# First attention: the order of the pairs' norms and of the last probabilities, and other banks

## The reference

```python
proj = x @ w_in
qa, ka, va, qb, kb, vb = split(proj)
qa, ka, qb, kb = rms_norm of each head (64 wide)
oa = dilated_mixture_attention(qa, ka, va, slopes[:8])        # 8 heads of 64
ob = differential_attention(qb, kb, vb, slopes[8:], lam)      # 4 heads; softmax 1 - lam * softmax 2
ob = rms_norm(ob, b_sub_norm) * (1.0 - lam_init)
y = concatenate([oa, ob]) @ w_out
```

## Time and profile before

| | |
|---|---|
| median of 3 runs | 2827.79 us (2825.66 to 2828.16) |
| time of the profiled execution | 2825.41 us |
| its span | 2823.6 us |
| PE busy in the span | 2793.2 us, 99% |
| DVE, ACT and POOL busy | 44% each |

### The profile page before, as it was taken

The page is one execution under the profiler, slowest core; times in us unless marked ns, Lnnn a source line. Parts: engine busy times, 40 slices in busy tenths (PEclk is TensorE's granted clock), DMA queues, the critical chain, the costliest instruction groups (busy, mean ns, idle before and its releaser), DMA issues.

```text
span 2823.6 us, 32514 instructions
## 1 busy us (share of the span) xinstructions
PE 2793.2 (99%) x12994; PEld 2267.7 (80%) x12994; DVE 1243.2 (44%) x2085; ACT 1231.8 (44%) x1805; POOL 1232.8 (44%) x549
## 2 busy tenths in 40 slices
PE   9999999999999999999999999999999999999998
PEld 8776888888878888887777888888877778888887
DVE  5666552544665525327666432021266574320112
ACT  4665442434754334334674443133345744342331
POOL 4222444444554444443455444444434564444442
PEclk9999999999999999999999999999999999999999
DMA  4212323233223332332222323333332222333332
GB/s 152 89 57 64 97 90 105 91 103 97 90 82 105 97 97 91 104 97 83 76 68 83 104 91 98 97 96 98 104 90 75 68 82 90 97 97 97 97 97 75
DMA packets 74215, 259.23 MB, mean 92 GB/s; under 512 B 9344, under 2 KB 9344, under 8 KB 74064
## 3 DMA queue, kind: packets, MB, share of 16 engines
q1 hardware_dynamic: 72768, 255.05, 29.0%
q10 hardware_dynamic: 1296, 2.10, 0.2%
HBM read 254.95 MB, written 2.13 MB: 91 GB/s over the span
## 4 chain that ended last, share of the span: by engine, by line
PE 94%; DVE 3%; ACT 2%; POOL 1%; issue 1%; DMA 0%; DVEq 0%; ACTq 0%; POOLq 0%
PE ps L427 27%; PE ps L429 27%; PE ps L428 27%; PE ps L493 2%; PE ps L523 2%; PE ps L549 1%; PE ps L506 1%; PE ps L551 1%; PE ps L550 1%; PE ps L475 1%; PE ps L477 1%; PE ps L476 1%; PE ps L438 1%; POOL w_lo L1988 0%; DVE pbuf L1457 0%
## 5 line engine op out<-in xcount | busy, mean ns | idle before, releaser
L1988 POOL TENSOR_TENSOR w_lo<-raw,w_hi 128x1024 fp32r<-128x1024 f32 x469 | 1132.9, 2418 | 1473.9 <-ACT w_hi L907 1473.8
L427 PE MATMUL ps<-xs,w_hi 128*128 128x512 f32 x2176 | 861.7, 396 | 1.6 <-DVE xs L1392 1.6
L429 PE MATMUL ps<-xs,w_lo 128*128 128x512 f32 x2176 | 847.1, 389 | 0.0
L428 PE MATMUL ps<-xs,w_hi 128*128 128x512 f32 x2176 | 847.0, 389 | 0.0
L907 ACT ACTIVATE w_hi<-raw 128x1024 fp32r<-128x1024 f32 x470 | 494.2, 1052 | 598.6 <-PE ps L429 555.6
L427 PE MATMUL ps<-hid,w_hi 128*128 128x512 f32 x1320 | 517.4, 392 | 7.7 <-DVE hid L1377 3.5
L429 PE MATMUL ps<-hid,w_lo 128*128 128x512 f32 x1320 | 514.4, 390 | 0.0
L428 PE MATMUL ps<-hid,w_hi 128*128 128x512 f32 x1320 | 514.2, 390 | 0.0
L427 PEld LDWEIGHTS ps<-xs,w_hi 128*128 128x128 f32 x2176 | 408.5, 188 | 101.1 <-issue 11.4
L428 PEld LDWEIGHTS ps<-xs,w_hi 128*128 128x128 f32 x2176 | 408.6, 188 | 88.7 <-issue 5.2
L429 PEld LDWEIGHTS ps<-xs,w_lo 128*128 128x128 f32 x2176 | 408.4, 188 | 85.5
(11 more groups left out here) (230 smaller groups left out, 2614.8 us busy)
## 6 DMA issues: line engine op xcount, KB each, us to landing
raw<-in_weights SPq DMA_DIRECT2D x470, 512.0 KB, 3.5
btab<-in_rel SPq DMA_DIRECT2D x8, 256.0 KB, 3.8
out<-tmp ACTq DMA_DIRECT2D x8, 256.0 KB, 2.0
hT<-in_x SPq DMA_DIRECT2D x3, 512.0 KB, 7.8
btab<-in_heads SPq DMA_DIRECT2D x6, 256.0 KB, 3.8
tmp<-in_heads SPq DMA_DIRECT2D x6, 256.0 KB, 4.1
common<-in_fixed SPq DMA_DIRECT2D x1, 642.0 KB, 11.0
hT<-in_x SPq DMA_DIRECT2D x2, 256.0 KB, 3.7
```

What stands on the lines that cost most here:

```text
L427: pe.matmul(banks[bank][:], wh, rh, start=(k == 0), stop=False)
L428: pe.matmul(banks[bank][:], wh, rl, start=False, stop=False)
L429: last = pe.matmul(banks[bank][:], wl, rh, start=False, stop=(k == len(specs) - 1))
L1988: gp.tensor_tensor(w_lo[:, n % NPAIR, :], raw[:, n % NRAW, :], w_hi[:, n % NPAIR, :].bitcast(F32), ALU.subtract).then_inc(*w_low.tick(n))
```

## The change

The edit is in the list of steps alone; no instruction is added or dropped.

- `before0`: `qk_turn` of pairs 0 and 1 comes ahead of the last `qk` step of the next pair.
- Pairs 3 to 7: the root is put at the end of the block before (`behind0[2]`, `[5]`, `[9]`, `[17]`, `[21]`), the norm is the first of the `beside` part in blocks 3, 6, 10, 18 and 22, ahead of the block's `qk` or `vb` step. The transposes stay in blocks 4, 7, 11, 19 and 23.
- `pair_banks` of pairs 4 to 7, `vb_banks` and `out_banks` are other banks.
- The `sublow` of unit 6, due in block 33, comes after `turn` and `unturn` of block 31 (`held`).
- The output matmuls (0 to 2, chunk 6) move behind `mix` of unit 7, those of (3 and 4, chunks 5 and 6) behind its `submean`.

```diff
--- before.py
+++ after.py
@@ -276,14 +276,15 @@
                 if 0 <= n - 1 < n_blocks:
                     steps.append(("weigh", n - 1))
                 steps += beside.get(n, [])
-                steps += due
+                held = due if n == n_blocks + LAG - 1 else []
+                steps += [] if held else due
                 if n >= LAG:
                     steps.append(("turn", n - LAG))
                     if late is not None:
                         steps.append(("mix", late))
                         later += ends_of(stage, late)
                         late = None
-                    steps.append(("unturn", n - LAG))
+                    steps += [("unturn", n - LAG)] + held
                     if (n - LAG) % NB == NB - 1:
                         late = (n - LAG) // NB
                 steps += (behind or {}).get(n, [])
@@ -305,42 +306,53 @@
 
 
         pairs = [(0, 0), (1, 0), (0, 1), (1, 1), (2, 0), (3, 0), (2, 1), (3, 1)]
-        pair_banks = [(5, 6), (7, 2), (5, 6), (7, 4)] + [((6, 7), (5, 6), (7, 5))[p % 3] for p in range(4)]
-        vb_banks = {(0, 0): 7, (0, 1): 6, (1, 0): 5, (1, 1): 6}
+        pair_banks = [(5, 6), (7, 2), (5, 6), (7, 4), (5, 6), (7, 5), (6, 7), (5, 6)]
+        vb_banks = {(0, 0): 6, (0, 1): 5, (1, 0): 7, (1, 1): 5}
 
         def unit_steps(p):
             return [("qk", (p, i, j)) for i in range(2) for j in range(2)]
 
         def vb_steps(half):
             return [("vb", (half, i, j)) for i in range(2) for j in range(2)]
-
-        def behind_next(p, after):
-
-            return [[after[0], ("qk_root", p)], [("qk_norm", p), after[1], ("qk_turn", p)], [after[2]], [after[3]]]
 
         before0 = unit_steps(0)
         for p in range(2):
             after = unit_steps(p + 1)
-            before0 += after[:1] + [("qk_root", p), ("qk_norm", p)] + after[1:] + [("qk_turn", p)]
+            before0 += after[:1] + [("qk_root", p), ("qk_norm", p)] + after[1:3] + [("qk_turn", p)] + after[3:]
+
+
+        beside0, behind0 = {}, {}
         after = unit_steps(3)
-        parts0 = [[after[0]], [after[1], ("qk_root", 2)], [("qk_norm", 2), after[2]], [after[3], ("qk_turn", 2)]]
-        for p, after in ((3, unit_steps(4)), (4, unit_steps(5)), (5, vb_steps(0))):
-            parts0 += behind_next(p, after)
-        parts0 += [[f] for f in unit_steps(6)] + behind_next(6, unit_steps(7))
-        beside0 = {}
-        for i, part in enumerate(parts0):
-            beside0.setdefault(0 if i < 2 else i - 1 if i < 6 else i - 2, []).extend(part)
+        beside0[0] = [after[0], after[1], ("qk_root", 2)]
+        beside0[1] = [("qk_norm", 2), after[2]]
+        beside0[2] = [after[3], ("qk_turn", 2)]
+        for p, n, after in ((3, 3, unit_steps(4)), (4, 6, unit_steps(5)), (5, 10, vb_steps(0))):
+            behind0[n - 1] = [("qk_root", p)]
+            beside0[n] = [("qk_norm", p), after[0]]
+            beside0[n + 1] = [after[1], ("qk_turn", p)] + ([after[2]] if p == 3 else [])
+            beside0[n + 2] = [after[2 if p > 3 else 3]]
+            if p > 3:
+                beside0[n + 3] = [after[3]]
+        for i, f in enumerate(unit_steps(6)):
+            beside0[14 + i] = [f]
+        after = unit_steps(7)
+        behind0[17] = [("qk_root", 6)]
+        beside0[18] = [("qk_norm", 6), after[0]]
+        beside0[19] = [after[1], ("qk_turn", 6)]
+        beside0[20], beside0[21] = after[2:3], after[3:]
         last_vb = vb_steps(1)
-        beside0[22] = [last_vb[0], ("qk_root", 7), ("qk_norm", 7)]
+        behind0[21] = [("qk_root", 7)]
+        beside0[22] = [("qk_norm", 7), last_vb[0]]
         beside0[23] = [("qk_turn", 7), last_vb[1]]
         beside0[24], beside0[25] = last_vb[2:3], last_vb[3:]
-        out_banks = (5, 6, 7, 0, 1, 2, 4, 3)
+        out_banks = (7, 5, 6, 0, 1, 2, 4, 3)
         early0 = {26: [(0, 0, 4)], 27: [(1, 0, 4)], 28: [(0, 4, 5), (1, 4, 5)], 29: [(2, 0, 5)],
                   31: [(0, 5, 6), (1, 5, 6), (2, 5, 6)], 32: [(3, 0, 5)], 33: [(4, 0, 3)],
-                  34: [(4, 3, 5)] + [(o, 6, 7) for o in range(3)], 35: [(3, 5, 7), (4, 5, 7)], 36: [(5, 0, 7)], 37: [(7, 0, 7)]}
+                  34: [(4, 3, 5)], 35: [(o, 6, 7) for o in range(3)],
+                  36: [(3, 5, 7), (4, 5, 7), (5, 0, 7)], 37: [(7, 0, 7)]}
         for n, v in early0.items():
             beside0[n] = [("out", a) for a in v]
-        steps0 = attention_steps("first", 8, beside0)
+        steps0 = attention_steps("first", 8, beside0, behind0)
 
         def qk_ready(n):
```

## The result

The changed kernel took 2818.72 us (median of 7 runs, 2816.76 to 2819.05), the kernel before 2828.16 (7 runs, 2825.66 to 2829.15). The ratio is 0.9969, 95% interval 0.996 to 0.9978: 9.4 us by the medians and faster by more than 0.2% over the whole interval. The forecast was 2818.9 us, 8.9 us faster.

The account below looks back on a forecast made before the run. TensorE, busy 2793.2 of 2823.6 us, was taken as the bound. Gains of 0.93 + 0.74 + 5.67 + 0.18 + 1.39 = 8.9 us, taken from the median, gave 2818.9 us; range 2815 to 2824.5.

Parts of the forecast that it names:

- two charges for the late table: Deductions for bias tables issued later: 0.35 us at block 1's first scores, 0.15 us at block 3's bank.
- turns of pairs 0 and 1, table in time: Transposes of the first two pairs one piece earlier, hiding ACT's bank copy: 2 x 0.64 = 1.28 us gained.
- given back to the table: At block 1, PE arrives early and waits for the first minimum, whose bias table is later: 0.35 us lost.
- banks, block 3: Pair 4's first unit on bank 5 no longer waits for DVE's copy: 0.74 us gained, bounds 0 and 0.89.
- pair 3: Earlier root and norm end the transposes' wait in block 4, including that for bank 7: 1.66 us gained.
- pairs 4 and 5: Earlier root and norm end the transposes' waits in blocks 7 and 11: 1.25 us gained at each.
- pairs 6 and 7: Earlier norm at block 19's transposes, 1.51 us; ACT's copy sooner for block 24's scores, 0.18 us.
- tail: Unit 7's mix ahead of the seventh chunk's output matmuls shortens PE's wait for y: 1.39 us gained.
- half microsecond of idle for bank 4: Expected sign: unit 7's mix starts near 236 with about half a microsecond of idle on PE.
- The waits change names: PE outruns bank copies, table-bound minimum and bank 4; gain only 3.5 us, 2824.3 us; chance 0.22 with the next rival.
- The norm was never the cause: weigh's wait for exponentials sets the norm's end at pairs 3 to 6; gain 3.2 us, 2824.6; in the shared 0.22.
- Slower: Late head sums hold the moved root and ACT's queue in five blocks; 5.7 us slower, 2833.5 us; chance 0.04.

Follow-up runs that it names:

- control: The changed kernel without any edit, on a further chip; its trace has no wait for the bias table: 2816.72 us, ratio 0.9964.
- norm_only: Kernel before with only root and norm of pairs 3 to 7 moved; its own banks, transposes and tail: 2821.36 us, ratio 0.9982.
- norm_back: Changed kernel with root and norm of pairs 3 to 7 back at their old places: 2825.86 us, ratio 0.9995.
- loads_twice: Changed kernel with two one-column activations, forcing two more table loads, ahead of each root of pairs 3 to 7: 2824.6 us, ratio 0.9988.
- tables_first: Changed kernel with the first two bias tables' loads issued ahead of the slab loads of the first three pairs: 2816.79 us, ratio 0.9961.
- tail_back: Changed kernel with unit 6's last step and chunk 6's output matmuls back ahead of the last mix: 2820.01 us, ratio 0.9974.
- banks_back: Changed kernel with the banks of pairs 4 to 7, of the values and of the output as before: 2820.95 us, ratio 0.9978.
- banks_back_tables_first: Changed kernel with the old banks and the bias tables loaded ahead of the slab loads: 2818.91 us, ratio 0.9973.
- norm_back_tables_first: Changed kernel with the old root and norm places and the bias tables loaded ahead of the slab loads: 2822.4 us, ratio 0.9986.

## Why the prediction was right, and what was off

*Place of the gain.* Right. The kernel before is 9.34 us behind `control` after the tail; the prediction without its two charges for the late table (0.35 and 0.15 us) is 9.41. The parts match step by step:

| part | predicted us | measured us (lags) |
|---|---|---|
| turns of pairs 0 and 1, table in time | 1.28 | 1.16 |
| given back to the table | 0.35 | 0 in two profiles with early turns and these tables' place; 1.1 to 1.6 in five, 1.3 in the result's |
| banks, block 3 | 0.74 | 2.14 - 1.16 = 0.98 |
| pair 3 | 1.66 | 3.81 - 2.14 = 1.67 |
| pairs 4 and 5 | 1.25 each | 1.24 and 1.25 |
| pairs 6 and 7 | 1.51 and 0.18 | 1.71 together |
| tail | 1.39 | 1.34 |

*Starts and not idle time.* The 3.3 us of listed idle for the norm and the 0.34 us for bank 7 became 5.6 us of gain at pairs 3 to 6 (7.75 - 2.14). In `norm_only`, which keeps the wait for bank 7, that is 7.75 - 2.14 less 2.74 - 2.09, 4.96 us for the norm alone. By the idle sums, 8.53 less 2.34, the executions of the kernel before and of the result would differ by 6.2 us; the lags give 9.34 - 1.31 = 8.03.

*The mis-sized term: the 0.35 us given back by the bias table.* The forecast had the tables issued a third of a microsecond later; they were, by 37.75 - 37.46 = 0.29 us. What it did not see is that the second table's distance behind the first is not fixed: 1.08 us in the profile before, 0.67, 2.01 and 2.33 in three of the changed kernel. In the result's execution the table took back 1.30 us, so the early transposes and the table together brought 1.16 - 1.31 = -0.15 us and not 0.93. Under a PE that arrives early this spread counts; before, DVE's second minimum was over at 74.80, ahead of a PE that came at 76.

*Pair 3.* Its 1.66 us were right, and the norm, forecast in time by 0.7 us, was so by 0.9. But the cause was told as the place of the norm in DVE's queue alone; of the 1.02 us that the late norm cost there, up to 0.86 come from the scaling that stood beside POOL. How long such a stand is depends on where the two meet, as `norm_back` shows, and the prediction has no term for it.

*The banks.* 0.98 us for 0.74: the charge of 0.15 for a late table does not apply to an execution where it is in time, and a wait of 0.89 us costs 0.98 by starts. That this wait holds a stand of DVE beside POOL is not in the prediction either.

*The tail.* Right in its 1.39 us and in its half microsecond of idle for bank 4. What is not in it is that the old wait can bring a fall of the clock with it that costs 1.67 us. The start of the mix, "near 236", takes the whole 8.9 us from 244.78, the tail's own part too; without that part it would be 237.3, and the clock at the start (1.03) and the table (0.96 more than charged) bring it near the measured 239.23.

*The sum.* 8.9 us against 9.4 by the medians, but partly by luck: the profile of before lay 2.4 us below the median that the prediction used (2.8 below that of the seven runs), that of the changed kernel at its own median, so the two profiles differ by 6.6 to 6.7 us: 8.03 gained in the attention, 1.03 lost ahead of it to the clock, and 0.4 lost behind it. That the medians differ by more than these two profiles is not explained term by term; three measurements with ratios of 0.9964 to 0.9969 hold it.

*The rivals.* "The waits change names" did not happen at pairs 3 to 6: no 256-column matmul waits. Its waits for the table and for bank 4 came, and both were in the forecast. "The norm was never the cause" is refuted by `norm_only` (5.26 us in the trace with nothing else moved). "Slower" did not happen, but its price was wrong: I gave it 5.9 us of room and 8.8 us of lateness to lose 2.9 us per place, while `loads_twice` lost up to 2.1 us per place from 3.05 us of lateness. The place to look was not what the late instruction itself feeds but what stands behind it in the queue.

## What to carry to other kernels

A wait of the engine that sets the end is best priced by the distance between starts, stalled against unstalled: listed idle time showed here 3.6 us of 5.6. When a step is moved up in a queue, price what stands behind it in that queue, not only its own reader. A transfer that was hidden by the bottleneck's own lateness comes to the front when that goes, with its spread; issuing it earlier (`tables_first`) took its wait away and cost nothing in the trace. Where a small operation takes several times its usual length, look for what another engine runs at that moment, before its place in the queue gets the blame.

## What the runs showed of the hardware

*The clock after a pause.* After waits of 1.79 us (`tail_back`), 2.0 (`banks_back`) and 2.25 us (`norm_back`) the granted clock fell, down to 0.51 in the lowest of the windows shown behind such a wait (the 1.2 GHz level), and cost 1.67 us in `tail_back`. An estimate for the other two, what their passage lost beyond the same passage with the tables first and beyond the longer wait, is 4.24 - 2.03 - (2.25 - 1.44) = 1.4 us and 3.60 - 0.92 - (1.99 - 0.85) = 1.5 us. After the same 1.79 us in `norm_only` and in the kernel before (9.34 - 8.00 = 1.34 us at the tail) it did not fall, nor after 2.07 us in `loads_twice` (L450, 1.00 in all windows of 190 to 202 us). So the price of such a wait has two values, and undoing a part measured 1.3 or 3.0 us for the same step. What decides it stays open. The same fall near the start, while the first slabs arrive, cost about a microsecond in nine of the twelve profiled executions of the changed kernel and the variants and not in `control`, `norm_back` and `banks_back_tables_first`; a cause in the edit is not shown, since the instructions there are the same.

*DVE beside POOL.* A scaling of 128 x 512 took 0.49 us alone and 2.40 us when POOL's slab piece had started ahead of it, and a 128 x 16 operation took 0.17 us alone and 1.22 us beside such a piece. They ended 0.28 and 0.03 us behind POOL's piece (93.98 for 91.04 + 2.66 = 93.70; 87.83 for 85.45 + 2.35 = 87.80); the scalings of 2.30 and 1.35 us ended 0.28 us behind it too. The Trainium skill ("SBUF — State Buffer", SBUF: two separate sides) says that the port pair that the two share is an exclusive lock, held for the whole instruction, and that the other fully blocks; it names DVE operations in a two-port mode or with two SBUF inputs. The trace agrees: both operations stood until POOL was done, and an operation that had started first (90.99, ahead of 91.04) kept its 0.49 us. No run moved POOL's piece by itself, so the link is read from rows of several profiles and not from an experiment. What it makes of a kernel is that the length of a small DVE operation depends on where it meets POOL's piece: a scaling of the same size ahead of pair 3's norm took 1.35 us in the kernel before, 2.30 in `norm_back_tables_first` and 2.40 in `norm_back`.
